# A chunked scan in two directions: turned inverse moved to the other half, products of both directions in turn on four corners, work between levels reordered

## The reference

```python
def step(S, inp):
    r_t, w_t, k_t, v_t, a_t, b_t = inp
    sa = jnp.einsum('bhij,bhj->bhi', S, a_t)
    S = S * w_t[:, :, None, :] + sa[..., None] * b_t[:, :, None, :] + v_t[..., None] * k_t[:, :, None, :]
    y = jnp.einsum('bhij,bhj->bhi', S, r_t) if emit else None
    return S, y
S, ys = lax.scan(step, state0, xs, reverse=reverse)
```

## Time and profile before

| | us |
|---|---|
| median of 3 runs (lowest, highest) | 1910.61 (1906.76, 1911.60) |
| the profiled execution | 1910.46 |
| its span, first to last instruction | 1908.6 |
| TensorE busy in the span | 1849.5 |
| VectorE, ScalarE, GpSimd busy | 758.2, 484.8, 98.6 |

### The profile page before, as it was taken

How to read it: one execution, slowest core, us unless ns; L and a number is a source line. 1 busy time by engine, 2 the same in 40 slices (tenths; PEclk the granted TensorE clock), 3 DMA queues, 4 the chain that set the end, 5 groups by cost and what they waited for, 6 DMA issues and landing times.

```text
span 1908.6 us, 31050 instructions
## 1 busy us (share of the span) xinstructions
PE 1849.5 (97%) x13470; PEld 1464.3 (77%) x13470; DVE 758.2 (40%) x1551; ACT 484.8 (25%) x1016; POOL 98.6 (5%) x117
## 2 busy tenths in 40 slices
PE   8999999888889999999999999999999999999999
PEld 3344655788878788788888888887888888888888
DVE  1224425456544794757322000027947663120000
ACT  2112235333325213553202000032136422110000
POOL 0001400333210000000000000000000000000000
PEclk9999999999999999999999999999999999999999
DMA  8311300000024333432343343443434334434342
GB/s 318 144 44 66 123 32 1 3 4 4 4 114 155 132 135 130 139 128 109 133 140 124 135 163 144 154 155 124 143 130 150 129 119 146 143 131 170 139 173 92
DMA packets 33223, 225.38 MB, mean 118 GB/s; under 512 B 4672, under 2 KB 6080, under 8 KB 6336
## 3 DMA queue, kind: packets, MB, share of 16 engines
q1 hardware_dynamic: 33088, 223.40, 32.2%
HBM read 222.34 MB, written 1.05 MB: 117 GB/s over the span
## 4 chain that ended last, share of the span: by engine, by line
PE 91%; DVE 4%; ACT 2%; issue 1%; SPq 1%; POOL 0%; DMA 0%; DVEq 0%; ACTq 0%
PE PS L450 25%; PE PS L591 12%; PE PS L1571 8%; PE PS L629 8%; PE PS L618 8%; PE PS L610 8%; PE PS L1209 2%; PE PS L1510 1%; PE PS L1211 1%; PE PS L1186 1%; PE PS L463 1%; PE PS L1662 1%; DVE ring L1413 1%; PE PS L564 1%; PE PS L349 1%
## 5 line engine op out<-in xcount | busy, mean ns | idle before, releaser
L450 PE MATMUL PS<-arena,ring 128*128 128x272 f32 (+1 forms) x2176 | 498.1, 389 | 0.0
L450 PEld LDWEIGHTS PS<-arena,ring 128*128 128x128 f32 x2176 | 411.2, 190 | 77.2 <-issue 1.4
L591 PE MATMUL PS<-arena,ring 128*128 128x272 f32 (+1 forms) x1024 | 229.5, 386 | 2.1 <-DVE arena L1052 2.1
L591 PEld LDWEIGHTS PS<-arena,ring 128*128 128x128 f32 x1024 | 194.2, 190 | 35.9 <-DVE arena L1052 2.9
L844 DVE SCALAR_TENSOR_TENSOR arena<-arena,par 128x272 f32<-128x272 f32 (+1 forms) x480 | 214.8, 489 | 15.7
L610 PE MATMUL PS<-arena,ring 128*128 128x272 f32 (+1 forms) x704 | 163.8, 386 | 0.0
L618 PE MATMUL PS<-arena,ring 128*128 128x272 f32 (+1 forms) x704 | 163.8, 386 | 0.0
L1571 PE MATMUL PS<-arena,ring 128*128 128x512 f32 (+2 forms) x448 | 158.1, 513 | 1.7 <-DVEq L1862 1.7
L629 PE MATMUL PS<-arena,ring 128*128 128x272 f32 (+1 forms) x704 | 157.1, 386 | 1.1 <-issue 1.1
L629 PEld LDWEIGHTS PS<-arena,ring 128*128 128x128 f32 x704 | 133.6, 190 | 24.7 <-issue 1.9
L610 PEld LDWEIGHTS PS<-arena,ring 128*128 128x128 f32 x704 | 133.8, 190 | 22.9
(11 more groups left out here) (325 smaller groups left out, 1884.1 us busy)
## 6 DMA issues: line engine op xcount, KB each, us to landing
ring<-stream_dram SPq DMA_DIRECT2D x207, 1024.0 KB, 4.8
arena<-x_dram SPq DMA_DIRECT2D x1, 2048.0 KB, 11.4
cst<-const_dram SPq DMA_DIRECT2D x1, 1080.0 KB, 7.4
out_dram<-H SPq DMA_DIRECT2D x4, 256.0 KB, 2.2
cst<-const_dram SPq DMA_DIRECT2D x1, 912.0 KB, 17.2
arena<-stream_dram SPq DMA_DIRECT2D x1, 512.0 KB, 7.0
par<-param_dram SPq DMA_DIRECT2D x2, 177.0 KB, 10.8
c<-const_dram SPq DMA_DIRECT2D x1, 128.0 KB, 2.3
```

The source lines that it names most:

```text
L450: last = mm(PS[:, (m + f) % 4, nw], lslot(l, n, KD, 256)[:, k, P * f:P * f + P], NT[:, k, nw], start=k == 0, stop=k == KD - 1)
L591: last = mm(PS[:, i % 4, NQ], lslot(l, n, KD, 256)[:, k, P * (i % 2):P * (i % 2) + P], src[:, k, NQ], start=k == 0, stop=k == KD - 1)
```

## The change

Direction 1 keeps W (and P) of head h in the other half of the partitions, so its `level` and growth products use the corners that direction 0 leaves. `level` now issues both directions' products in turn, and `widen` is split: `grow` makes Z's part for both directions in turn, `grow_turned` makes W's part after it, and VectorE adds Z's 256 columns first (`grown`) and W's later (`grown_turned`). Value, state and output products of the two directions ride beside one another in `right_sides` and `outputs`. Reordered: sums and exps of the next chunk from level 3 to 1, `prepare` from 4 to 2, `turn` from 1 to 3, `products`, copy of A and first inverse from 5 to 4, outputs from 4 to 5. The scaling of the keys moves from VectorE's `prepare` to GpSimd. Removed lines of the old functions are left out where the functions print above.

```diff
             dve.wait_ge(S["exps_made"], n + 1)
-            ar, bk = AR[n % 3][:, d], BKF[:, d, :, c, :, :]
-            v.tensor_tensor(bk, bk, EX[:, d].unsqueeze(2).broadcast_to((P, 4, 2, CH)), ALU.mult)
+            ar = AR[n % 3][:, d]
             v.scalar_tensor_tensor(ar[:, :, 0, :], ar[:, :, 0, :], -1.0,
                                    KK[:, c // 4:8:2, CH * (c % 4):CH * (c % 4) + CH], ALU.mult, ALU.mult)
             v.tensor_tensor(ar[:, :, 1, :], ar[:, :, 1, :], SH[:, 0:4, heads(c)], ALU.mult).then_inc(S["prepared"], 1)
...
             mm = nc.tensor.matmul
             each = [(q, h) for q in range(4) for h in range(2)]
...
+                return halves(h if d == 0 else 1 - h)
             def products(n, d):
                 S, m, c = SCAN[d], n - 2, chunk_at(d, n)
...
                 pe.wait_ge(S["prepared"], n + 1)
+                pe.wait_ge(S["bk_ready"], n + 1)
                 if 0 <= m < NCH - 1:
                     pe.wait_ge(S["s_kept"], m + 1)
-                if m >= 4:
-                    pe.wait_ge(S["y_kept"], m - 3)
+                if n:
+                    pe.wait_ge(S["t_kept"], n)
...
                 S, c = SCAN[d], chunk_at(d, n)
...
+                if n:
+                    pe.wait_ge(S["u_kept"], n)
+                else:
+                    pe.wait_ge(S["exps_made"], 2)
                 for q in range(4):
                     last = nc.tensor.transpose(PS[:, 4 * d + 2, P * q:P * q + P],
                                                BKF[:, d, q, c, :, :].rearrange("p s t -> p (s t)"), ident)
                 last.then_inc(S["t_made"], 1)
...
+            def level(n, l):
+                for S in SCAN:
                     pe.wait_ge(S["xl_ready"], 5 * n + l)
                     pe.wait_ge(S["z_ready"], 5 * n + l)
...
+                    if l == 1 and n:
+                        pe.wait_ge(S["zf_ready"], n)
+                for q, h in each:
+                    for d in range(2):
+                        last = mm(PS[home(d, h), 4 * d, heads(q)], XL[halves(h), l - 1, d, q, :],
+                                  ZW[halves(h), n % 2, d, 0, q, :], start=True, stop=True)
+                        if (q, h) == (3, 1):
+                            last.then_inc(SCAN[d]["p_made"], 1)
+            def grow(n, l):
+                for S in SCAN:
+                    pe.wait_ge(S["p_kept"], 5 * n + l)
+                    pe.wait_ge(S["w_ready"], 4 * n + l - 1)
+                for q, h in each:
+                    for d in range(2):
+                        last = mm(PS[halves(h), 4 * d, heads(4 + q)], ZW[home(d, h), n % 2, d, 1, q, :],
+                                  P1[home(d, h), d, q, :], start=True, stop=True)
+                        if (q, h) == (3, 1):
+                            last.then_inc(SCAN[d]["dz_made"], 1)
+            def grow_turned(n, l, d):
+                S = SCAN[d]
+                if l == 1 and n >= 6:
+                    pe.wait_ge(S["y_kept"], n - 5)
+                if l == 2 and n >= 4:
+                    pe.wait_ge(S["r_kept"], n - 3)
+                for q, h in each:
+                    o = home(d, h)
+                    last = mm(PS[o, 4 * d + 1, heads(q)], P1[o, d, q, :], ZW[o, n % 2, d, 1, q, :], start=True, stop=True)
+                last.then_inc(S["dw_made"], 1)
+            def value(m, d, q, h):
+                o, S = halves(1 - h), SCAN[d]
+                if (q, h) == (0, 0):
                     pe.wait_ge(S["b_kept"], m + 1)
                     if m:
                         pe.wait_ge(S["s_kept"], m)
...
+                last = mm(PS[halves(h), 4 * d + 3, heads(q)], MKA[o, m % 2, d, q, :], VT[o, chunk_at(d, m), q, :],
+                          start=q == 0, stop=m == 0 and q == 3)
+                if (q, h) == (3, 1):
+                    last.then_inc(S["v_made"], 1)
+            def state_part(m, d, q, h):
+                S = SCAN[d]
+                if (q, h) == (0, 0):
+                    pe.wait_ge(S["v_made"], m + 1)
+                last = mm(PS[halves(h), 4 * d + 3, heads(q)], AR[m % 3][halves(h), d, q, 0, :],
+                          ST[halves(h), m % 2, d, q, :], start=False, stop=q == 3)
+                if (q, h) == (3, 1):
+                    last.then_inc(S["rh_made"], 1)
+            def output_product(n, d, q, h):
+                S, c = SCAN[d], chunk_at(d, n)
+                if (q, h) == (0, 0):
+                    pe.wait_ge(S["w_ready"], 4 * n)
+                    if n >= 6:
+                        pe.wait_ge(S["y_kept"], n - 5)
+                last = mm(PS[halves(h), 4 * d + 1, heads(4 + q)], BKF[halves(h), d, q, c, h, :],
+                          AR[n % 3][halves(h), d, q, 1, :], start=True, stop=True)
+                if (q, h) == (3, 1):
+                    last.then_inc(S["r_made"], 1)
+            def right_sides(n):
+                m = n - 1
                 for q, h in each:
...
+                    if m >= 0:
+                        value(m, 0, q, h)
+                    if 4 <= n < NCH:
+                        output_product(n, 0, q, h)
                 for q, h in each:
...
+                    if m >= 0:
+                        value(m, 1, q, h)
+                    if m >= 1:
+                        state_part(m, 0, q, h)
                 for q, h in each:
...
+                    if m >= 1:
+                        state_part(m, 1, q, h)
+                    if 4 <= n < NCH:
+                        output_product(n, 1, q, h)
             def solve(m, d):
                 S, par = SCAN[d], m % 2
...
+                pe.wait_ge(S["t_kept"], m + 1)
+                pe.wait_ge(S["exps_made"], min(m + 3, NCH))
                 pe.wait_ge(S["zf_ready"], m + 1)
                 pe.wait_ge(S["rh_kept"], m + 1)
@@ -1248,55 +1286,71 @@
...
+            def output_value(m, d, q, h):
+                S, o = SCAN[d], halves(1 - h)
+                if (q, h) == (0, 0):
+                    pe.wait_ge(S["w_ready"], 4 * min(m + 2, NCH))
+                    pe.wait_ge(S["r_kept"], min(m - 2, NCH // 2))
+                last = mm(PS[halves(h), 4 * d + 1, heads(4 + q)], VT[o, chunk_at(d, m), q, :], MRK[o, m % 2, d, q, :],
+                          start=q == 0, stop=False)
+                if (q, h) == (3, 1):
+                    last.then_inc(S["yv_made"], 1)
+            def output(m, d, q, h):
+                S, par, o = SCAN[d], m % 2, halves(h)
+                if (q, h) == (0, 0):
+                    pe.wait_ge(S["yv_made"], m - 3)
+                    pe.wait_ge(S["u_kept"], m + 1)
+                out = PS[o, 4 * d + 1, heads(4 + q)]
+                mm(out, ST[o, par, d, q, :], AR[m % 3][o, d, q, 1, :], start=False, stop=False)
+                last = mm(out, US[o, d, q, :], MRB[o, par, d, q, :], start=False, stop=q == 3)
+                if (q, h) == (3, 1):
+                    last.then_inc(S["y_made"], 1)
+            def outputs(m):
                 for q, h in each:
...
+                    output_value(m, 0, q, h)
+                for q, h in each:
+                    output_value(m, 1, q, h)
+                    output(m, 0, q, h)
+                for q, h in each:
+                    output(m, 1, q, h)
             for d in range(2):
                 products(0, d)
             for n in range(NCH + 1):
                 m = n - 1
                 for l in range(1, 6):
...
+                    if n < NCH:
+                        level(n, l)
+                    if l == 1:
+                        right_sides(n)
+                        if n < NCH - 1:
+                            for d in range(2):
+                                pe.wait_ge(SCAN[d]["b_kept"], n + 1)
+                            chunk_sums(pe, n + 1, (2, 6))
                     if l == 2 and m >= 0:
                         for d in range(2):
                             solve(m, d)
                     if l == 3 and 0 <= m < NCH - 1:
                         for d in range(2):
                             state_step(m, d)
...
+                    if l == 3 and n < NCH:
                         for d in range(2):
...
+                            turn(n, d)
+                    if l == 4 and n < NCH - 1:
                         for d in range(2):
                             products(n + 1, d)
+                    if l == 5 and m >= 4:
+                        outputs(m)
                     if n < NCH:
...
+                        grow(n, l)
+                        if l < 5:
+                            for d in range(2):
+                                grow_turned(n, l, d)
         def scalar_scan(act):
             a = nc.scalar.activation
...
+                    if l == 1 and n < NCH - 1:
+                        for d in range(2):
+                            chunk_exps(act, n + 1, d, 4 * d + 2)
...
+                            keep_first(n + 1, d)
+                    if l == 5 and m >= 4:
                         for d in range(2):
```

(55 more changed lines are left out.)

120 lines of the change are left out of this document (14 added, 106 removed).

## The result

The changed kernel takes 1916.86 us (median of 11 runs, 1911.31 to 1923.22) beside 1911.02 (1906.76 to 1915.74) for the kernel before: ratio 1.0038, 95% interval 1.0022 to 1.0055. It is 5.8 us slower; 1887 was forecast, 30 us less. The profiled execution has a span of 1912.6 us.

A forecast was written before the change was run, and what follows sets the result against it. The scan's hand-offs were taken as the bound, TensorE being the fullest engine, and after the change the chain of waits. From 1910.5 us, 26.8 gained in the scan and 3.3 lost to the clock gave 1887.0; range 1876 to 1900.

The forecast's parts named there:

- Four corners take 0.50 us a group: Both directions' level products, and both directions' growth products, each form one group on four array corners: 0.50 us where 0.93 stood.
- rival E: The array corners take turns, so each of 80 joined groups costs 0.43 us more: 1918, slower; chance 0.03.
- The bare level gains nothing: A scan level with nothing else issued in it takes 3.41 us after the change against 3.44 before.
- Level 3: Third level of a chunk, with state step and turns as filler, 0.9 us beyond the free room: 4.3 us.
- Products wait for the state, VectorE's block of 4 us holds level 5: Level 4's next-chunk products wait for the new state, 5.5 us; level 5's last adds wait for first inverses, 5.55 us.
- The clock, 3.3 us: Five 3.3 us idle stretches before level 1 may drop TensorE to half rate: 0 to 8.5 us, 3.3 taken.
- The prediction's dear end: The largest clock loss allowed for level 1 after the five idle stretches, 8.5 us, for a total of 1892 us.
- The chain is then the bound: TensorE's work per scan chunk falls from about 23 to about 19 us, so the chain of waits sets the time.
- Joining gains room: In each level TensorE has 1.27 us free for other work between the last level product and growth.
- Rival D: No gain: each of 80 joined groups waits 0.3 us longer for the slower direction, 24 us: 1908; chance 0.05.
- The outputs are hidden in level 5: Outputs end their growth at 4.4 us of level 5; a full chunk takes 24.0 us with or without them.
- Keys on GpSimd and writes across halves cost nothing: Key scaling on GpSimd, some 1.4 us twice a chunk, and VectorE's products written across halves were taken to add 0.

## Why the prediction was wrong, step by step

The forecast and the profiles, by parts of the scan. Chunk 0 is counted with the later start of its first copy (2.5 us, in the third column 2.95). The third column is the changed kernel with its clock filled in chunks 0 to 4.

| | forecast | after | clock filled |
|---|---|---|---|
| chunk 0 | 22.05 | 25.0 | 25.6 |
| chunk 1 | 23.0 | 25.25 | 24.4 |
| chunks 2, 3 | 48.0 | 58.6 | 49.8 |
| chunks 4 to 6 | 72.0 | 85.4 | 77.2 |
| chunk 7 and rest | 25.1 | 28.3 | 28.4 |
| level 1, chunks 2, 3, 4 | 5.25 | 6.84, 7.47, 7.12 | 5.33, 5.33, 5.86 |
| level 2 | 3.4 | 4.91, 4.33, 3.71 | 4.54, 4.38, 3.71 |
| level 3 | 4.3 | 4.22, 4.40, 4.22 | 4.22, 4.20, 4.23 |
| level 4 | 5.5 | 7.35, 6.78, 6.94 | 5.53, 6.23, 5.64 |
| level 5 | 5.55 | 6.09, 6.25, 6.00 | 5.37, 4.70, 5.97 |

- *Four corners take 0.50 us a group*: right: 32 passes from 345.39 to 345.88, so rival E's price is not paid. *The bare level gains nothing*: right (3.28). *Level 3*: right to 0.1. *Products wait for the state, VectorE's block of 4 us holds level 5*: right, both rows are above. (The turned growth "0.93 x 2" is a slip of the prediction: its own count of work has 0.93 for both directions, and its sums use that.)
- *The clock, 3.3 us*: this term was mis-sized, by a factor of two at the least. The clock fell in level 1 of the chunks it was forecast for, but three times for 6.8 us and not 3.4, and once more in chunk 0. Level 1 of chunks 2 to 4 is 1.3 to 2.1 us longer than with the clock kept, and over chunks 1 to 5 it is 6.6 us, the least that the clock cost. Filling brought 0.0081, 15.5 us, which is too much for the clock alone: of the 17.2 us between the two profiles 4.7 fell where no fill stands and the clock was full. So the clock's share lies between 6.6 and about 13 us, an estimate from these levels. The Trainium skill, "TensorE: Matmul & The Clock Gate", part 1, says that the slow clock is the default state which activity releases; the trace agrees, with 30.7 us at half clock. The prediction's dear end, 8.5 us (1892), lies within what was measured.
- *"The chain is then the bound"*: this step failed. It takes for granted that TensorE's instructions are always there; the price for that was put at nothing. It was read from groups of 0.5 us, and a hint was in the trace of before: `issue` waits behind a landing, and one instruction block every 4 to 5 us. The denser a group is issued, the shorter the 100 instructions of lead last. In level 4 of chunks 2, 3 and 4 stood 1.75, 1.55 and 1.44 us of it, about the distance from 5.5 to 7; where no stand-still fell into it (third column, chunk 2) the level took 5.53. Level 2 took 3.71 where none fell into it (chunk 4), and 4.33 and 4.91 with waits of 0.75 and 1.52. By place alone the stand-stills moved the time by 0.0026 and 0.0036.
- *Joining gains room*: the room was there and brought no time: two corners in turn are 5 to 6 us faster (0.0025 to 0.0031), with fewer stand-stills and less half clock. Rival D (each group waits for the slower direction, 1908) names a wait that exists, but no run prices it by itself; rival E (corners take turns, 1918) has the sign and nearly the time by luck, since its mechanism is refuted by the passes.
- *The outputs are hidden in level 5*: right in chunks 5 and 6, to 0.2 us. The 6.3 us that three quarters of them were worth lie in chunk 7 and the rest, forecast at 25.1 us and measured at 28.3.
- *Keys on GpSimd and writes across halves cost nothing*: right (1.0042 against 1.0038; 0.42 us a piece).

The prices overlap and don't sum to 30 us: what fills an idle stretch also spreads the issue. Shown, each by a run of its own, are that the clock costs, that the stand-stills do and that their price depends on place, that joining gains nothing, and that the outputs of the last chunk are on the path. With the clock kept, the parts of the scan still sum to 15 us more than the forecast (205.4 beside 190.2), so the clock is about half of the miss at most. Open stay the clock's exact share, what in joining costs, and how much of the time is lost to stand-stills in all, since their sum doesn't follow the time from kernel to kernel.

## What to carry to other kernels

Before counting on denser issue, count instructions: in rows of many small products look for idle time that ends in `issue`, and hold it against the instruction queue's packets. Packing work so that an engine idles may cost its clock, and a queue's order on the engine that it waits for (here one line on VectorE) was worth 16 us, 1.0038 to 0.9954, nearly three times what the whole change lost. Dummies that hold the clock pay only where the engine would stand idle: beside work that fills it they are work. A variant a per cent apart from another is best run again with the code shifted by half a block and by a whole one.

## What the runs showed of the hardware that was not expected

- A dense stream of 64x64 float32 products gets 256 instructions per 3.5 to 4.0 us, of which it issues for 2.1; a block landed in 0.9 to 1.4 us and in the stream TensorE went on 1.2 to 1.5 us later.
- 256 instructions without effect ahead of the scan change nothing (1.0042), 128 change 0.0026.
- In the changed kernel the clock fell six times, each time at a wait of TensorE of 2.5 us or more: at 415.0 within the 3.26 us ahead of 415.63, at 384.2 already 0.6 us into one, at 339.9 only 1.0 us behind one. It came back 3.4 or 6.8 us later, so most of the half clock lay on the work behind the wait.
- A stretch with 102 passes in 6.9 us at 0.51 held 166 (6 of them dummies) in 7.0 at 1.00 once dummies of 128 by 256 kept TensorE at work. 32 dummies of 2 by 2 per chunk did not do that: 37.4 us of that scan are at half clock, beside 30.7 without them.
